# Two transformer blocks on one Trainium2 core: layer 1 on the input tokens alone, the attention output in three passes, and another order in the router

## The reference, cut to what matters

```python
for l in range(DEPTH):                                   # first_block, DEPTH = 2
    h = rmsnorm(h_res, norm_gain[l])
    proj = h @ w_in[l]
    u_pool, z_pool, c_q, c_kv, k_rope, z_mla, g_pool, g_mla = jnp.split(proj, IN_SPLIT_POINTS, axis=-1)
    y_pool = (pool_mix(u_pool, pool_w_group[l], pool_scale[l]) * jax.nn.silu(z_pool)) @ pool_w_up[l]
    o_mla = mla(c_q, c_kv, k_rope, pos, ...)
    y_mla = (o_mla * jax.nn.silu(z_mla)) @ mla_w_up[l]
    merged = jax.nn.sigmoid(g_pool) * y_pool + jax.nn.sigmoid(g_mla) * y_mla
    h_res = h_res + merged @ w_out[l]
return h_res[:, N_META:]
```

```python
o = diff_attention(q, k, v, lam)
o = rms_norm(o, attn_subln_gain[l]) * (1.0 - lam_init)
attn_d = jnp.einsum('bsc,cd->bsd', o.reshape(B, S, ATTN_WIDTH), w_attn_o[l])
xr = centred_depthwise_conv(lru_x, conv_w[l], conv_b[l])
h_fwd, h_bwd = rg_lru(xr, ..., False), rg_lru(xr, ..., True)     # two recurrences over the tokens
y_lru = (h_fwd + h_bwd) * jax.nn.gelu(lru_g)
lru_d = jnp.einsum('bsc,cd->bsd', y_lru, w_lru_o[l])
g_attn, g_lru = jnp.split(jax.nn.sigmoid(gate_pre + b_gates[l]), N_GATED_BRANCHES, axis=-1)
x = x + jnp.einsum('bsd,de->bse', g_attn * attn_d + g_lru * lru_d, w_out[l])
h2 = rms_norm(x, norm2_gain[l])
x = x + hierarchical_moe(h2, ...)      # 4 groups of 4 experts, the best group, its best 2 experts
```

## Time and profile before

| | us |
|---|---|
| median of 3 runs | 1833.78 (1833.67 to 1835.75) |
| span of the profiled execution | 1830.6 |
| PE busy | 1762.0 (96%) |
| PE weight loads busy | 1504.5 (82%) |
| DVE busy | 1187.4 (65%) |
| ACT busy | 875.0 (48%) |
| POOL busy | 331.4 (18%) |
| mean granted PE clock | 0.988 of full speed |

### The profile page before, as it was taken

The page is one execution under the profiler, slowest core; times in us unless marked ns, Lnnn a source line. Parts: engine busy times, 40 slices in busy tenths (PEclk is TensorE's granted clock), DMA queues, the critical chain, the costliest instruction groups (busy, mean ns, idle before and its releaser), DMA issues.

```text
span 1830.6 us, 27554 instructions
## 1 busy us (share of the span) xinstructions
PE 1762.0 (96%) x11270; PEld 1504.5 (82%) x11270; DVE 1187.4 (65%) x1704; ACT 875.0 (48%) x1407; POOL 331.4 (18%) x223
## 2 busy tenths in 40 slices
PE   8999999999999999999999999999999989999993
PEld 6998788999998888999999776765568867888882
DVE  5566645554366655544676598586764457888896
ACT  5425444234334444334343365556553246878771
POOL 3333222002243222001000276310010000000001
PEclk9999999999999999999999999999999989999997
DMA  6203112223312202323222210213142359999994
GB/s 188 76 24 99 47 47 79 84 70 116 96 59 75 70 25 69 100 93 98 93 83 80 69 47 24 67 48 99 63 172 93 115 195 346 403 402 404 403 384 173
DMA packets 156104, 241.46 MB, mean 132 GB/s; under 512 B 9593, under 2 KB 101018, under 8 KB 155978
## 3 DMA queue, kind: packets, MB, share of 16 engines
q1 hardware_dynamic: 148602, 212.88, 33.9%
q0 software_dynamic: 4464, 16.25, 2.3%
q10 hardware_dynamic: 2912, 10.55, 1.4%
HBM read 223.41 MB, written 16.25 MB: 131 GB/s over the span
## 4 chain that ended last, share of the span: by engine, by line
PE 51%; DVE 5%; ACT 4%; issue 1%; DMA 1%; POOL 0%; POOLq 0%; ACTq 0%; DVEq 0%
PE acc L1358 15%; PE acc L856 10%; PE acc L1101 9%; PE acc L1126 7%; PE acc L1190 2%; PE acc L1204 2%; PE acc L1221 1%; PE acc L1344 1%; PE acc L1212 1%; PE acc L1086 1%; DVE upad L2681 1%; DVE qk L2681 0%; ACT v L1954 0%; PE acc L1008 0%; DVE qk L2679 0%
## 5 line engine op out<-in xcount | busy, mean ns | idle before, releaser
L856 PE MATMUL acc<-h_split,ring_split 128*128 128x264 f32 x1088 | 308.2, 283 | 0.0
L856 PEld LDWEIGHTS acc<-h_split,ring_split 128*128 128x128 f32 x1088 | 204.3, 188 | 0.0
L856 PE MATMUL acc<-h_split,qk_split 128*128 128x264 f32 x384 | 109.5, 285 | 1.3 <-DVE ring_split L2188 1.3
L856 PE MATMUL acc<-ring_split,qk_split 128*128 128x264 f32 x384 | 108.8, 283 | 0.0
L1126 PE MATMUL acc<-ring_split,h_split 128*128 128x256 f32 x384 | 107.9, 281 | 0.0
L856 PE MATMUL acc<-h_split,krope_split 128*128 128x264 f32 x320 | 93.4, 292 | 1.7 <-POOL ring_split L3010 1.6
L856 PE MATMUL acc<-ring_split,krope_split 128*128 128x264 f32 x320 | 90.7, 284 | 0.0
L2188 DVE TENSOR_TENSOR ring_split<-ring,o_split 128x1024 fp32r<-128x1024 f32 (+1 forms) x32 | 44.8, 1417 | 65.3 <-ACT o_split L1520 65.1
L3120 POOL DMA_INDIRECT latent<-h_rows,rows_of x16 | 18.1, 1129 | 355.8 <-PE acc L1344 214.1
L2188 DVE TENSOR_TENSOR ring_split<-ring,qk_split 128x1024 fp32r<-128x1024 f32 (+1 forms) x56 | 59.4, 1070 | 34.1 <-ACT qk_split L1520 34.1
L2996 POOL TENSOR_TENSOR latent<-latent 128x528 f32<-128x528 f32 x18 | 26.8, 1490 | 300.1 <-ACT latent L1515 299.8
(11 more groups left out here) (597 smaller groups left out, 5741.4 us busy)
## 6 DMA issues: line engine op xcount, KB each, us to landing
ring<-in_w_in SPq DMA_DIRECT2D x64, 1024.0 KB, 5.2
ring<-in_w_expert_gate SPq DMA_DIRECT2D x10, 2048.0 KB, 13.7
ring<-in_w_expert_up SPq DMA_DIRECT2D x10, 2048.0 KB, 13.9
ring<-in_w_expert_down SPq DMA_DIRECT2D x10, 2048.0 KB, 14.7
ring<-in_w_out SPq DMA_DIRECT2D x12, 1024.0 KB, 5.0
y_rows<-gate ACTq DMA_DIRECT2D x16, 512.0 KB, 6.8
hres<-in_w_expert_up SPq DMA_DIRECT2D x3, 2048.0 KB, 12.9
qk<-in_w_expert_down SPq DMA_DIRECT2D x3, 2048.0 KB, 14.5
```

The costliest lines, as they stand in the source:

```text
L856: ins = nc.tensor.matmul(dst[0:rows_, half, 0:HALF], w[:, k, :], x[:, c], start=(k == 0 and i == 0), stop=(k == last and i == 2), skip_gro ...
```

## The change

Three changes come together.

1. **Layer 1 on input tokens.** New helpers `wanted`, `bank` and `passes` give, in the last layer, for the jobs named in `NARROW` and for c < QC, one bank of 512 columns (tokens 16 to 527) where two halves of 264 were. ACT, DVE and POOL instructions on these results take the same 512 columns. POOL's memset of the meta columns goes.
2. **Attention output in three passes.** ya(m) becomes `product3` over on_up (fp32r copies by ACT, in `qk_split`) and on_low (by DVE, in `hres_split`, which overlays the residual xr). on(c) is written to a temporary, then halved. The weights of ya now have to be halved too: they join JOBS_2 between the ga jobs, upper half by ACT, lower half by POOL. SP stores xr (2 MB) to the DRAM tensor `x_kept` ahead of the granule q2, and loads it back ahead of gl3, after ya(7).
3. **Router.** ACT squares each residual chunk as out2 makes it (sq3), POOL sums seven of them, and PE turns the sums into columns by two sets of four one-column matmuls; the turns of x into tokens move behind the turns of h2 (0, 1) and behind rows_of (2, 3), all evicted by ACT. Places are five fp32r matmuls, rows_of is fp32r; the shares of the softmax move behind rows_of, and the weights of the choice to the first expert.

The diff, cut to its core:

```diff
+        def wanted(x, narrow=True):
+
+            return x[:, META:T] if narrow and on_input() else x.rearrange("p (a t) -> p a t", a=2)
...
+        def passes(dst, x, narrow=True):
+
+            if narrow and on_input():
+                return [(dst[:, 0, :], x[:, META:T])]
+            return [(dst[:, half, 0:HALF], x[:, half * HALF:(half + 1) * HALF]) for half in range(2)]
+
+        NARROW = ("z", "pg", "gp", "yp", "zm", "gm", "ym", "out")
+
+        def narrow_job(label):
+
+            return label[0] in NARROW or (label[0] == "c" and label[1] < QC)
...
+        on_up, on_low = m2_up, [hres_split[:, c, 0:S] for c in range(DC)]
...
                   + [(("lg", c), f"lg{c // 2}", c % 2) for c in range(DC)]
-                  + [(("ga", m), f"ga{m // 2}", m % 2) for m in range(DC)]
+                  + [x for m in range(DC) for x in ((("ga", m), f"ga{m // 2}", m % 2), (("ya", m), f"ao{m // 2}", m % 2))]
...
-        LOW_BY_POOL = [job_no2["lx", c] for c in range(4, DC)]
+        LOW_BY_POOL = [job_no2["lx", c] for c in range(4, DC)] + [job_no2["ya", m] for m in range(DC)]
...
+                if name == "q2":
+                    sp.wait_ge(dve_made, at(dve_made, ("h2low", DC - 1)))
+                    sp.dma_start(x_kept, xr).then_inc(x_away, 16)
+                elif name == "gl3":
+                    sp.wait_ge(psum_filled, at(psum_filled, ("ya", DC - 1)))
+                    sp.wait_ge(x_away, 16)
+                    sp.dma_start(xr, x_kept).then_inc(x_back, 16)
...
-                        for i, (w, x) in enumerate(((w1, up[k]), (w1, low[k]), (w0, up[k]))):
-                            ins = nc.tensor.matmul(dst[0:rows_, half, 0:HALF], w[:, k, :], x[:, c],
+                    narrow = narrow_job(label)
+                    for (to, of_up), (_, of_low) in zip(passes(dst, up[k], narrow), passes(dst, low[k], narrow)):
...
                 product3(("ga", m), dve_evacuated, h2_up, h2_low)
-                if m % 2 == 0:
-                    weights2_in(f"ao{m // 2}")
-                product2(("ya", m), dve_evacuated, [columns2(f"ao{m // 2}", m % 2)[:, k, :] for k in range(DC)],
-                         lambda k: q2[:, k, :],
-                         before=(lambda k: pe.wait_ge(dve_made, at(dve_made, ("on", k)))) if m == 0 else None)
+                product3(("ya", m), dve_evacuated, on_up, on_low,
+                         before=(lambda k: pe.wait_ge(dve_made, at(dve_made, ("onlow", k)))) if m == 0 else None)
...
-            x_turn(0)
+            def token_squares(x, first=False):
+
+                for i in range(QT):
+                    ins = nc.tensor.matmul(to_logits[:, 1, i:i + 1], x[:, i * P:(i + 1) * P], ones[:, 0:1],
+                                           start=first and i == 0, stop=not first, skip_group_check=True)
+                return ins
+
+            pe.wait_ge(pool_made, at(pool_made, "sum3"))
+            token_squares(squared2[0], True)
             for k in range(4, DC):
                 ins = router_product(to_logits, k)
             done(ins, "logits")
-            x_turn(1)
+            pe.wait_ge(squared, at(squared, ("sq3", DC - 1)))
+            done(token_squares(squared2[DC - 1]), "ss_2")
...
-            x_turn(2)
-            x_turn(3)
...
                 done(ins, ("h_tok", i))
-
+            x_turn(0)
+            x_turn(1)
...
+            pe.wait_ge(dve_made, at(dve_made, "lt"))
+            chosen = R_split[:, R_M:R_M + 64]
+            nc.tensor.matmul(dst[:, 0, 0:64], lt_split, chosen, start=True, stop=False,
+                             skip_group_check=True)
+            for i in range(1, QT + 1):
+                ins = nc.tensor.matmul(dst[:, 0, 16 * i:80], ones_split, chosen[:, 0:80 - 16 * i], start=False,
+                                       stop=(i == QT), skip_group_check=True)
...
             done(ins, "rows_of")
+            x_turn(2)
+            x_turn(3)
...
+            def normed_upper(c):
+
+                act.wait_ge(dve_made, at(dve_made, ("on", c)))
+                upper(on_up[c], tmp[2 + c % 2], ("onup", c))
...
                     if i >= 2:
-                        act.wait_ge(dve_made, at(dve_made, ("on", i - 2)))
+                        normed_upper(i - 2)
+                        act.wait_ge(dve_made, at(dve_made, ("onlow", i - 2)))
...
+            for c in range(DC - 2, DC):
+                normed_upper(c)
...
+                weights2_upper(job_no2["ya", m] + 2)
...
+                    nc.scalar.activation(small[:, 14:15], small[:, 1:2], ACT.Sqrt)
+                act.wait_ge(dve_evacuated, at(dve_evacuated, ("out2", m)))
+                nc.scalar.activation(squared2[m], xr[:, m, :], ACT.Square).then_inc(squared, 1)
+                mark(squared, ("sq3", m))
...
                 act.dma_start(y_rows[e * P:(e + 1) * P, :], y_out).then_inc(y_main, 16)
 
-            for j in range(4):
+            for j in range(2):
                 weights_up(j)
+            act.wait_ge(dve_made, at(dve_made, "shifted"))
+            made(nc.scalar.activation(R[:, R_X:R_X + 80], R[:, R_X:R_X + 80], ACT.Exp), "shares")
+            x_kept_by_token(2)
+            x_kept_by_token(3)
+            weights_up(2)
             expert_turned(0)
-            for j in range(4, 6):
...
-                if c + LAG < DC:
+                if c + LAG < DC - 1:
                     weights2_lower(job_no2["lg", c + LAG] + 2)
                 if c < 0:
                     continue
                 inverse2(("oss", c), 2 + c % 2)
                 if c == 0:
                     chain(ts(small[:, 13:14], vec2[:, V_SUB:V_SUB + 1], 1.0 - LAM_INIT, None, ALU.mult))
-                made(stt(out=q2[:, c, :], in0=q2[:, c, :], scalar=small[:, 13:14], in1=tmp[2 + c % 2],
-                         op0=ALU.mult, op1=ALU.mult), ("on", c))
+                x = tmp[2 + c % 2]
+                made(stt(out=x, in0=q2[:, c, :], scalar=small[:, 13:14], in1=x, op0=ALU.mult, op1=ALU.mult), ("on", c))
+                if c == 0:
+                    dve.wait_ge(x_away, 16)
+                lower(on_low[c], x, on_up[c], ("onlow", c), ("onup", c))
...
                         if u == 2 * DC - 3:
+                            weights2_lower(job_no2["gl", 1])
                             gate_in(("gl", 0), DC)
...
+            for m in range(DC):
+                weights2_lower(job_no2["ya", m])
 
```

258 lines of the change are left out of this document (137 added, 121 removed).

## The result

| | before | after |
|---|---|---|
| median | 1834.76 us (4 runs, 1833.67 to 1836.3) | 1872.97 us (4 runs, 1872.54 to 1873.36) |
| ratio | | 1.0211, interval 1.0197 to 1.0226 |
| span of the profiled execution | 1830.6 | 1871.2 |
| mean granted PE clock | 0.988 | 0.973 |

A forecast was written before the change was run, and what follows sets the result against it. It took TensorE, busy 96% of the span, as the bound, with VectorE and ScalarE just behind in places. Terms -12.5 + 31.3 + 6 + 1 + 0.5 - 4.5 = +21.8 gave 1855.6 us, range 1842 to 1868.

The forecast's parts named there:

- What bounds the kernel: Whole kernel: TensorE is busy 96% of the span; in attention output and gate loop VectorE and ScalarE stand just behind.
- Narrow passes, -12.5: Layer 1: 1104 pairs of 264-column matmuls become single ones of 512, saving 11.3 ns each, 12.5 us.
- The waits, +31.3: Attention output: +20.2 us up to the end of ya(0), +11.1 in the gate loop; gl(0) starts 31.3 late.
- The clock, +6: Attention output and gate loop: half clock behind some seven idles of 3.3 to 4.8 us costs 6 us.
- bound of 9.5: Clock loss with 3.4 us at half clock behind each idle, playing the queues again: 9.5 us.
- VectorE against POOL, +1: Gate loop: seven POOL subtractions of 2.40 us slow VectorE by 1 us, bounds 0 and 16.8.
- Rival C: Gate loop: POOL blocks VectorE, 5 to 15.8 us more, 1861 to 1871; chance 0.09.
- Keeping xr, +0.5: Storing the residual, 2 MB, ahead of the q2 weights delays them; costs 0.5 us, bounds 0 and 2.
- Router, -4.5: From the last out2 to the first expert: a gain of 2 to 8 us, taken as 4.5.
- (A): Attention output and gate loop: the queues hide all waits, the loop follows TensorE, -27.3 us, 1806.5; chance 0.06.
- (B): The clock stays up, the rest as forecast: 1849.6, or 1846 with the router's 8 us; chance 0.2.
- (D): Attention output and gate loop: a third of the 31.3 us isn't there, as hand-overs overlap more: 1845; chance 0.1.

The follow-up runs named there:

- e13: The whole change with ya's lower weight halves made by VectorE instead of POOL, and filler matmuls, three ahead of ga(3), ga(5), ga(7): 1854.59 us.
- e10: The kernel before with narrow passes and router part, and ScalarE making the experts' fourth weight half ahead of the first expert's turned tokens: 1814.25 us.
- e4: The kernel before with the narrow passes and the router part together, the attention output as before: 1819.35 us.
- e6: The whole change with ScalarE's upper half of on(c) taken one iteration earlier: 1851.22 us.
- e5: The whole change with filler matmuls that nothing reads ahead of TensorE's long waits, five ahead of ga(3), ga(5), ga(7): 1863.10 us.
- e7: As e6, and in the gate loop ScalarE's upper half of ya's next weights stands behind the four square roots: 1848.86 us.
- e9: The whole change with ya's lower weight halves made by VectorE instead of POOL, and filler matmuls, five ahead of ga(3), ga(5), ga(7): 1860.72 us.
- e12: As e5, with three instead of five filler matmuls ahead of ga(3), ga(5), ga(7): 1861.81 us.
- e11: The whole change with the early upper half of on(c) and filler matmuls, those ahead of lg(5), lg(6), lg(7) left out: 1847.58 us.
- e1: The kernel before with the narrow passes of layer 1 (512 columns) alone: 1821.08 us.

## Why the prediction was wrong, point by point

The forecast was 18.8 us short, span against span (+40.6 for +21.8). By its own terms: POOL 7.7, router 3.2, clock 2.4, the gl stage 2.4, experts to the end 1.5, stage waits 1.5, layer 1 0.6, and 0.5 too much for xr; together 18.8. POOL's share of these alone is more than the 5 us by which the median lies outside the range.

**What bounds the kernel**: right. The change lost its time where VectorE and ScalarE stood just behind TensorE, and gained where TensorE alone bounds.

**Narrow passes, -12.5**: 13.4 alone, 11.9 at lg(0) in the whole change. Right. The estimate from the start-to-start time that the Trainium skill gives (TensorE: Matmul & The Clock Gate, section "Wait — 56ns, not 53.3ns?") was 10.2; the trace doesn't agree: 231.2 ns for 512 columns against 215.8, and 12.4 ns saved a pair against 9.2.

**The waits, +31.3**: right in place and cause, and nearly in size. The idles of 3.3 us before lg(5), (6), (7) were 3.31, 3.24, 3.24; the early upper half removed them (21.8 of 22). Without clock and POOL the stage cost 35.3, where the same working gives 33.8: some 19.6 up to the end of ya(0), where 20.2 were forecast, and 15.7 behind it, where 11.1 were forecast and 2.5 come with VectorE's subtractions. In the change itself the two parts were 29.4 and 20.5.

**The clock, +6**: undersized. About 8.4 us or more up to gl(0), near the bound of 9.5. That the bound came near is in part luck: it took seven idles with 3.4 us at half clock behind each, 24 us together, where the stage had some 51, and taking away some 41 of these gave no more than 8.4. The reason given for less, "part of the loss is taken up by later waits", took the same thing off twice: the 9.5 came from playing the queues through, and that holds what later waits take up.

**VectorE against POOL, +1: the step that failed.** The edit from fillers alone to fillers with VectorE's subtractions shortened the stage by 6.2 us, and it added 2.5 of VectorE's own work by the played-through orders, so POOL cost some 8.7. This is an estimate: the 2.5 is no measurement, and the clock rose in the same step (0.98 to 1.00 over the stage). The step with equal clocks, 4.0 us but with fillers that were too long, gives 6.5. VectorE's rows hold enough for either: eight of its instructions beside POOL's eight subtractions lasted 10.7 us longer than their like, three pairs 2.2 each, the chunk's lower half 2.0, one scaling 1.1, three products 1.1 together. The eighth POOL subtraction, ahead of ya(0), wasn't in the forecast at all; the wait before the last sum of squares was 4.40 for it instead of 2.5. I had the row (1.80 instead of 0.75) and both bounds, and took the low one because POOL's subtraction "falls mostly where VectorE waits". It doesn't: in ScalarE's queue the copies that VectorE's pair waits for stand right ahead of the weight half that releases POOL, so POOL began 0.3 us into the pair in three of the four even m (m = 0 has no such pair). The rule of the exclusive lock (the Trainium skill, SBUF — State Buffer, section "SBUF: two separate sides") agrees with the rows: the stretched instructions end 0.3 to 0.6 us behind POOL's. Rival C had the mechanism, at a chance of 0.09, and its 5 to 15.8 us above the forecast's 1 hold the 5.5 to 7.7 found; I hadn't joined it with the clock's upper bound.

The stage sums: 31.3 (waits) + 8.4 (clock) + 8.7 (POOL) = 48.4 of 49.9; 1.5 is left, as e13 had 1.5 over its working. The terms are the steps from run to run, so this sum is no test of them. The 2.4 us behind gl(0) I had left out; the idle of 2.3 ahead of gl(1) lies there, but no run took it alone. The 1.5 us from the first expert to the end go with the idle before it: in the profiles of every run with 3 us of idle or more there this part is 317.4 to 319.5 long, in those with 1.1 or less 316.2 to 316.6. Half clock behind that idle is the likely reason (0.72 from 1546 to 1558 us in the change); the edit of e10, which takes the idle away, brought it from e4's 319.0 to 316.2.

**Keeping xr, +0.5**: TensorE's waits from 880 to 1160 us are those of the kernel before, 5.2 us in all, and lg(0) starts where it does in e4, which stores nothing (1150.48 and 1150.57). Right, even nothing.

**Router, -4.5**: 1.3 in the whole, 2.1 alone, under even the lower bound of 2 in the whole. The step that failed here is "the last two token turns stand between rows_of and the experts": they did, at the forecast time, but what came last was the fourth weight half behind the gathered tokens in ScalarE's queue, and the half clock behind that idle. I had the two orders and didn't follow VectorE's queue to its end. With that half moved the router part gives 6.0 to 6.8 (13.4 to 19.5 below the kernel before; 1821.08 to 1814.25, on two chips).

**The rivals.** (A) is out: every idle came. (B) is out: the clock fell. (D) is out: the waits were all there. The range failed because POOL was taken near the good end of its bounds, with a row at the bad one, and because the clock, the router and the parts behind gl(0), smaller errors, all went the same way.

## What to carry to other kernels

A step that turns an fp32 product into three cheaper passes adds two operands to prepare on other engines; price it by the ring of those engines, not by the matmuls saved, and where it hands a result from VectorE to ScalarE and back, look at what stands ahead of the hand-over in both queues: one iteration too late cost 22 us here. Idle time of TensorE costs more than itself when the clock falls behind it, and in a ring of waits that price is only partly hidden: here, taking away some 41 of 51 us at half clock gave 8.4 us. Work given to POOL isn't free of VectorE: when both read and write SBUF, a POOL instruction of 2.4 to 2.6 us put up to 2.2 us onto a pair of VectorE's that takes 1.3.

## What the runs showed of the hardware

The same wait can leave the clock up or not. TensorE's wait near 1030, in code that no edit touches, was 1.95 us in the change and in e6. In the timeline and the stretch behind it the change has

```profile
1029.73 0.44 PE L1247 MATMUL acc<-const,gate 128*128 128x128 f32 x2 [1.95 <-DVE gate L2700]
...
1030.00:1035.00 5.00, 4.03 (x23) 2.49 (x22) 4.86 (x7) 1.94 (x5) 4.72 (x4) 1.00 0.00 0
```

and e6

```profile
1030.51 0.61 PE L1247 MATMUL acc<-const,gate 128*128 128x128 f32 x2 [1.95 <-DVE gate L2700]
...
1030.00:1035.00 5.00, 4.49 (x14) 2.39 (x14) 4.86 (x8) 1.94 (x5) 4.72 (x4) 0.66 0.00 0
```

with a clock of 0.66 over 5 us. It fell there in the profiles of e5, e7, e9, e10 and e12 too, but not in e11. In the same way a wait of 2.3 us near 577 was followed by a fall in the kernel before (0.83 from 574 to 584 us) and by none in e1 (1.00).

VectorE's product with a PSUM operand wasn't stretched beside POOL (0.68 us), while instructions on SBUF operands alone that began during a POOL subtraction were, a scaling with one such operand too (1.55 instead of 0.49). One that was already running when POOL began wasn't.
